# A mixture-of-experts decoder step on one core: expert inputs selected by matmuls on chip, and three visits with 64 places

## The chip, the core and the metric

The kernel runs on one core of a Trainium2 chip. The core has a matrix engine (PE, with PEld for its weight loads), a vector engine (DVE), a scalar engine (ACT), GpSimd (POOL) and SyncE (SP), and 16 DMA engines that all queues share. The metric is the device time of one execution in microseconds (us). A piece of weights here is 2048 KB or less, and a "visit" is the work of one expert.

## The reference

One step of a two-layer decoder on 256 prompt tokens and 8 sample tokens (264 in all, width 1024): retention and a dense SwiGLU, then an HGRN2 mixer and a top-2-of-8 expert SwiGLU with hidden width 3584. All is fp32. The change lies in the expert part:

```python
def moe_swiglu(h, router, wg, wu, wd):
    probs = jax.nn.softmax((h @ router).astype(F32), axis=-1)
    vals, idx = lax.top_k(probs, TOP_K)
    vals = vals / jnp.sum(vals, axis=-1, keepdims=True)
    combine = jnp.sum(jax.nn.one_hot(idx, N_EXPERTS, dtype=F32) * vals[..., None], axis=-2)
    out = jnp.zeros(h.shape, F32)
    for e in range(N_EXPERTS):
        out = out + combine[..., e:e + 1] * swiglu(h, wg[e], wu[e], wd[e]).astype(F32)
    return out.astype(h.dtype)
```

Here h is the RMS-normed row with a gain. Over the reference's inputs the router chooses the eight experts 74, 68, 61, 70, 66, 55, 72 and 62 times (528 choices).

## The kernel before

**The mixers.** The first 683 us compute both mixers and the dense layer with the tokens along the free dimension. The last product there (`hw`) adds into `xT`; PE turns `xT` back into token rows `x_tok` (`finished_rows`) and forms the router's logits, DVE chooses two experts a token, and PE counts, by a triangular matmul, the place of each token within its expert (`rk`).

**The visits.** A visit holds C = 96 places (TG = 3 groups of 32) for the tokens of one expert, the last visit only 64 (two groups, `GROUPS`); DVE puts the least-chosen of the experts 1 to 7 into the last visit (`order_of_visits`). If an expert has more tokens than places, all eight visits are repeated in another round of the loop `Fori(0, rounds)`; the trace shows one round. A visit (loop over `e`) uses 24 pieces of weights in the order of `EXPERT`: pieces 0 to 15 are gate and up, in two halves of the hidden width, of 1792 KB each; pieces 16 to 23 are the down projection, three of 2048 KB and one of 1024 KB in each half. `rows_times` multiplies `xe` (the expert's inputs, turned so that channels lie on partitions, 8 x 96 places) by a gate or up piece: 2 k-slices x groups x 4 matmuls of 32 columns, four at a time in the array. `hidden_times` does the same with `hide` and a down piece. ACT applies silu (L1312), DVE multiplies (L1947) and turns the hidden rows (L1949). Each fp32 matmul stands as two rows in the trace.

**The weights.** SP loads the pieces into 8 slots (`MOE_SLOT`). Before a piece it waits until PE is done with the piece eight earlier (`reused`, semaphore `w_used`). Piece 18 of the last visit is loaded ahead during visit 1, into a place of its own (`ahead_slot`).

**The expert inputs.** For visit 0, PE selects rows by matmuls (36 of them, `gsel` as weights, 256 columns of `x_tok` moving), DVE multiplies by the gain (L1907) and turns them (L1899). For the other visits DVE writes normed rows `h_tok` (`normed_rows`, L1894), POOL scatters each token's row to its two places of the DRAM tensor `y_scr` (L962, six indirect DMAs), SP loads 128 rows of it for the next visit (`load_rows`, L832, at piece 12 of a visit, or piece 2 of the last), and DVE turns them in blocks of 32 x 256 (L1954, 8 or 12 a visit) at the end of the visit.

**The results.** ACT and DVE take a visit's result out of PSUM in the next visit (L1303, L1941) and ACT stores it in `y_scr`. After piece 17 of the last visit POOL gathers two rows a token (L969, `w_seen`); DVE adds them by weight (`early`, L1969). The last visit's result goes from PSUM to tokens by a selection matmul (`select`), DVE adds it (`late`, L1976), and `final` norms and scales the rows (L1986), which SP stores.

Of the kernel before, what the change touches and what calls it, by code (L numbers as in the profile page):

```python
# [48 lines left out]
C_LAST = 64  # L49
GROUPS = [TG] * (NE - 1) + [C_LAST // 32]  # L50
# [248 lines left out]
def hybrid_step(nc, ins, outs):  # L299
    FILL, BANKS = fills()  # L300
    with ExitStack() as ctx:
# [42 lines left out]
        sel_mem = sb("last_selection", [P, 896], F32R)  # L344
# [112 lines left out]
        h_tok = part(earena, 3072, 3, D)  # L457
        gsel = part(earena, 6144, 3, C)
        ahead_slot = earena[:, 3072:3072 + PIECE]
        act_g = part(earena, 7168, TG, GW)  # L460
        first_rows = part(earena, 7168, TG, 256)

        y_out = part(cst, CONST["ones"][0], TG, 512)
        g_row = cst[:, CONST["lvl"][0] - 128:CONST["lvl"][1]]
        frees_at = 9264
        gfin = cst[:, CONST["dmask"][0]:CONST["dmask"][1]]
        x_row = g_row
        xe = part(xe_mem, 0, KD, C)

        g_group = part(hide_mem, 384, 1, 256)  # L470
        hide = [part(hide_mem, h * HB * C, HB, C) for h in range(2)]
        squares_at = [h_tok[:, 0, :], xe_mem[:, 0:D], hide_mem[:, 0:D]]
# [20 lines left out]
        last_sel = part(sel_mem, 0, TG, NT)  # L493
# [8 lines left out]
        oab = part(earena, RB + 184, 2, 3, 8)  # L502
# [6 lines left out]
        counts = part(earena, RB + 452, 8)  # L509
        visit_8 = part(earena, RB + 460, 8)  # L510
        visit_of = part(earena, RB + 500, 2, 3)
        to_last = part(earena, RB + 506, 2)
# [54 lines left out]
        x_pad_ok = sem("sample_rows_padded")  # L567
        h_tok_ok = sem("normed_rows_ready")
# [26 lines left out]
        x_scattered = sem("x_rows_scattered")  # L595
        x_row_in = sem("expert_x_rows_in")
        xe_ok = sem("expert_x_ready")
        gate_ok = sem("expert_silu_ready")
# [181 lines left out]
        X_AT, X_AT_LAST = 12, 2  # L780
# [20 lines left out]
        def _(sp):  # L801
# [29 lines left out]
            def load_rows(i):  # L831
                sp.dma_start(x_row, y_scr[bass.ds(i * C, P), :]).then_inc(x_row_in, 16)  # L832

            for t in range(EP):
                if t == X_AT:
                    sp.wait_ge(x_scattered, 96)
                    load_rows(2)
# [21 lines left out]
            def visit(v, i):  # L859
# [34 lines left out]
        def _(pool):  # L894
# [53 lines left out]
            freed(pool, ("lv", 4, 3))  # L948
            pool.dma_start(g_row, ins["norm_ffn_g"][1].partition_broadcast(P)).then_inc(rows_in, 16)
            filled(pool, ("hvar", 0))  # L950
            for c in range(4):
                pool.dma_start(g_group[32 * c:32 * c + 32, 0, :],
                               ins["norm_ffn_g"][1][256 * c:256 * c + 256].partition_broadcast(32)).then_inc(rows_in, 16)
# [390 lines left out]
        def _(dve):  # L1344
# [568 lines left out]
            for t in range(3):  # L1913
                normed_rows(t)
# [742 lines left out]
```

## Time and profile before

| | us |
|---|---|
| median of 3 runs | 1541.55 (1540.8 to 1542.12) |
| the profiled execution | 1543.34 |
| its span in the trace | 1541.5 |
| start of visit 0 in it | 682.6 |
| visits 0 to 7 | 682.6 to 1526.7 |
| after the last product of visit 7 | 14.8 |

The page shows PE busy for 98% of the span, over half of it in the visits, where the DMA engines are busy too. The rows of a visit repeat, so one visit can be read for several. A matmul's row overlaps its neighbours', so that the pace of PE is read from starts, not from the length of one row. "issue" means that the engine waited for nothing that the profile shows.

### The profile page before, as it was taken

What the parts mean: (1) busy time and instruction counts of PE and PEld (TensorE: products, weight loads), DVE (VectorE), ACT (ScalarE), POOL (GpSimd) and SP (SyncE); (2) the same over time, 40 slices, a digit from 0 to 9 for tenths busy, and PEclk for the clock granted to TensorE, in tenths of its full rate; (3) what the DMA queues carried; (4) which work ended last, traced back from release to release, by engine and by line L of the source; (5) the groups of instructions that cost most, each with busy time, mean ns of one, the idle gap of its engine ahead of it and who ended that gap; (6) DMA issues with size and microseconds to landing.
All of it is one profiled execution on the core that took longest, in us unless ns stands there. A gap on an engine that the chain in (4) does not pass through costs nothing.

```text
span 1541.5 us, 31601 instructions
## 1 busy us (share of the span) xinstructions
PE 1511.2 (98%) x14136; PEld 903.7 (59%) x14136; DVE 643.9 (42%) x1025; ACT 404.6 (26%) x613; POOL 86.6 (6%) x118
## 2 busy tenths in 40 slices
PE   9999999999999999999999999999999999999986
PEld 7888889999999999864333333333333333333322
DVE  7566878677656897551301301301311312112034
ACT  4444666544455547530000010010010000000001
POOL 1122221000000011010000000000000000000001
PEclk9999999999999999999999999999999999999998
DMA  9687786688656545569999999999999999999995
GB/s 373 223 287 268 258 291 216 201 275 280 223 179 209 199 164 196 233 234 418 426 408 427 426 425 427 424 419 429 405 424 430 395 423 427 401 427 416 423 427 249
DMA packets 136937, 515.88 MB, mean 335 GB/s; under 512 B 6488, under 2 KB 58912, under 8 KB 128480
## 3 DMA queue, kind: packets, MB, share of 16 engines
q1 hardware_dynamic: 116672, 450.03, 73.7%
q0 software_dynamic: 15968, 57.97, 10.2%
q10 hardware_dynamic: 4160, 5.84, 1.1%
q8 instruction: 112, 1.84, 0.4%
q14 instruction: 25, 0.20, 0.0%
HBM read 473.48 MB, written 40.34 MB: 333 GB/s over the span
## 4 chain that ended last, share of the span: by engine, by line
issue 53%; PE 37%; DVE 3%; ACT 1%; DMA 1%; POOL 0%; POOLq 0%; ACTq 0%; DVEq 0%
PE ps L2020 35%; DMA ring<-y_scr,expert_arena 1%; PE ps L2233 1%; DVE ring L1458 0%; POOL y_scr L962 0%; ACT ring_low_parts L1019 0%; DVE expert_arena L1969 0%; PE ps L2360 0%; DVE expert_arena L1986 0%; DVE ring_low_parts L1408 0%; DVE expert_arena L1976 0%; DVE expert_arena L1894 0%; ACT arena L1196 0%; PE ps L2481 0%; DVE arena L1748 0%
## 5 line engine op out<-in xcount | busy, mean ns | idle before, releaser
L2020 PE MATMUL ps<-ring,expert_x_turned 128*32 128x448 f32 x5152 | 488.8, 539 | 1.6 <-issue 0.8
L2020 PEld LDWEIGHTS ps<-ring,expert_x_turned 128*32 128x32 f32 x5152 | 169.5, 110 | 318.1 <-issue 316.2
L2020 PE MATMUL ps<-normed_high,ring_low_parts 128*128 128x264 f32 x1344 | 267.2, 290 | 0.4 <-DVE normed_low L1392 0.4
L2020 PE MATMUL ps<-ring,expert_hidden_turned 128*32 128x512 f32 x2360 | 257.4, 595 | 6.0 <-DMA ring<-in_moe_w_down 6.0
L1408 DVE TENSOR_TENSOR ring_low_parts<-ring,ring_low_parts 128x1024 fp32r<-128x1024 f32 (+3 forms) x184 | 209.1, 1142 | 84.6 <-ACT ring_low_parts L1019 84.2
L1019 ACT CAST ring_low_parts<-ring 128x1024 fp32r<-128x1024 f32 (+3 forms) x184 | 180.8, 983 | 222.9 <-PE ps L2020 214.3
L1947 DVE TENSOR_TENSOR expert_arena<-expert_arena,ps 128x1344 f32<-128x1344 f32 (+1 forms) x16 | 23.9, 1496 | 481.8 <-PE ps L2020 481.8
L2020 PEld LDWEIGHTS ps<-normed_high,ring_low_parts 128*128 128x128 f32 x1344 | 214.9, 189 | 5.4 <-issue 4.2
L2020 PEld LDWEIGHTS ps<-ring,expert_hidden_turned 128*32 128x32 f32 x2360 | 76.8, 110 | 184.0 <-issue 174.4
L2020 PE MATMUL ps<-normed_low,ring_low_parts 128*128 128x264 f32 x640 | 159.3, 284 | 0.0
L2020 PE MATMUL ps<-h_parts,ring_low_parts 128*128 128x264 f32 x1056 | 129.6, 285 | 0.0
L2020 PEld LDWEIGHTS ps<-h_parts,ring_low_parts 128*128 128x128 f32 x1056 | 129.0, 188 | 0.5 <-issue 0.4
L2020 PEld LDWEIGHTS ps<-normed_low,ring_low_parts 128*128 128x128 f32 x640 | 120.6, 188 | 0.6 <-issue 0.2
L1303 ACT COPY cst<-ps 32x1536 f32<-32x1536 f32 (+1 forms) x16 | 22.1, 1378 | 370.4 <-PE ps L2020 370.1
L1312 ACT ACTIVATE expert_arena<-ps 128x1344 f32<-128x1344 f32 (+1 forms) x16 | 19.9, 1244 | 365.9 <-PE ps L2020 365.9
L1941 DVE TENSOR_TENSOR cst<-ps,cst 32x1536 f32<-32x1536 f32 (+1 forms) x16 | 26.9, 1684 | 182.9 <-ACT cst L1303 182.1
L2020 PE MATMUL ps<-mixed_high,ring_low_parts 128*128 128x264 f32 x384 | 74.6, 291 | 1.7 <-DVE normed_high L1793 1.6
L2020 PE MATMUL ps<-expert_piece_slot,expert_x_turned 128*32 128x448 f32 x736 | 72.1, 539 | 1.1 <-DMA expert_piece_slot<-in_moe_w_up 1.1
L2020 PE MATMUL ps<-hidden_high,ring_low_parts 128*128 128x264 f32 x352 | 64.2, 284 | 0.0
L2020 PEld LDWEIGHTS ps<-mixed_high,ring_low_parts 128*128 128x128 f32 x384 | 61.0, 191 | 4.0 <-issue 2.5
L1954 DVE STREAM_TRANSPOSE expert_x_turned<-cst 32x256 f32<-32x256 f32 x92 | 58.8, 639 | 1.1
L2020 PEld LDWEIGHTS ps<-hidden_high,ring_low_parts 128*128 128x128 f32 x352 | 54.5, 188 | 0.0
(294 smaller groups left out, 1157.0 us busy)
## 6 DMA issues: line engine op xcount, KB each, us to landing
ring<-in_moe_w_gate SPq DMA_DIRECT2D x64, 1792.0 KB, 12.0
ring<-in_moe_w_down SPq DMA_DIRECT2D x47, 2048.0 KB, 13.6
ring<-in_moe_w_up SPq DMA_DIRECT2D x48, 1792.0 KB, 12.2
expert_piece_slot<-in_moe_w_up SPq DMA_DIRECT2D x16, 1792.0 KB, 13.0
ring<-in_ret_w_in SPq DMA_DIRECT2D x8, 2048.0 KB, 11.1
ring<-in_state_retention POOLq DMA_DIRECT2D x32, 512.0 KB, 6.6
out_ret_s<-ring POOLq DMA_DIRECT2D x32, 512.0 KB, 4.0
ring<-in_hg_w_in SPq DMA_DIRECT2D x8, 2048.0 KB, 8.0
```

The lines of the kernel that those rows point to most:

```text
L1019: A.copy(block_hi(n), block_raw(n)).then_inc(fw_hi_ok, 1)
L1303: A.copy(y_out[64 * q:64 * q + 32, 0:m], ps[64 * q + 32:64 * q + 64, b:b + m, :]).then_inc(y_half_ok, 1)
L1312: A.activation(act_g[:, 0:m], ps[:, b:b + m, 0:GW], ACT.Silu).then_inc(gate_ok, 1)
L1408: V.tensor_tensor(block_lo(n), block_raw(n), block_hi(n).bitcast(F32), ALU.subtract).then_inc(fw_lo_ok, 1)
L1941: V.tensor_tensor(y_out[z, 0:m], ps[z, b:b + m, :], y_out[z, 0:m], ALU.add).then_inc(y_ok, 1)
L1947: V.tensor_tensor(act_g[:, 0:m], act_g[:, 0:m], ps[:, b:b + m, 0:GW], ALU.mult).then_inc(mult_ok, 1)
L1954: j = V.transpose(xe[32 * c:32 * c + 32, :, 32 * t:32 * t + 32], x_row[32 * t:32 * t + 32, 256 * c:256 * c + 256].rearrange("p (f b) -> p ...
L2020: return nc.tensor.matmul(out, lhsT, rhs, start=first, stop=last)
L2233: i = nc.tensor.transpose(bank(("vb", u))[:, P * e:P * e + P], col, ident)
```

## The change

The inputs of every visit are now formed as those of visit 0 were, by matmuls on chip, and already turned.

- **gather_x on PE.** 24 matmuls (8 channel slices x 3 blocks of tokens): the weights are 128 columns of `x_tok`, taken eight elements (32 bytes) apart, the moving operand is the selection `gsel` (96 or 64 places). For visit 0 they replace the 36 of before. For every next visit, and after visit 7 too, they stand behind piece 17 of the visit (`GATHER_BEHIND`), into PSUM banks 6 and 7.
- **DVE.** `selection` (three small operations) after the first hidden half of each visit, and `take_expert_x` (two multiplies by the gain, out of PSUM) at its end, in place of the 8 or 12 transposes. The ranks of all experts are kept (`rank_at`), and `order_of_visits` swaps three pairs of columns of a table of ten numbers an expert.
- **Gone.** `normed_rows`, the six scattering DMAs, the row loads of SP and its wait for the scatter, the two loads of gain rows (one small load of the gain instead), a fill of `x_tok` on POOL.
- **64 places in three visits.** `FEW = (7, 4, 1)`: visits 1, 4 and 7 hold the three least-chosen of experts 1 to 7 (55, 61 and 62 tokens) with two groups in place of three. Another round is run if the third of them has over 64.
- A shorter `keep_busy` after visit 0's selection, and a wait of PE for `xe_ok` before the final selection.

```diff
-C_LAST = 64
-GROUPS = [TG] * (NE - 1) + [C_LAST // 32]
+C_FEW = 64
+FEW = (7, 4, 1)
+GROUPS = [C_FEW // 32 if v in FEW else TG for v in range(NE)]
...
-                    if t == (X_AT if v < NE - 1 else X_AT_LAST):
-                        sp.wait_ge(xe_ok, i + 1)
-                        load_rows(i + 2)
...
-            pool.wait_ge(h_tok_ok, 3)
             pool.wait_ge(rows_ok, 1)
-            pool.wait_ge(xe_ok, 1)
-            for t in range(3):
-                m = P if t < 2 else NS
-                for w in range(2):
-                    pool.indirect_dma_start(y_scr[:, :], bass.IndirectOffsetOnAxis(ap=rowi[0:m, w, t:t + 1], axis=0),
-                                            h_tok[0:m, t, :], None).then_inc(x_scattered, 16)
...
+            def selection(v, numbers):
+
+                for t in range(3):
+                    m = P if t < 2 else NS
+                    i = V.tensor_scalar(gsel[0:m, t, 0:32 * GROUPS[v]], numbers[0:m, 0:32 * GROUPS[v]],
+                                        rank_at[0:m, t, v:v + 1], rstd_tok[0:m, t:t + 1], ALU.is_equal, ALU.mult)
+                i.then_inc(sel_ok, 1)
...
+                for n, v in enumerate(FEW):
+                    link(V.tensor_scalar(swap_at, expert_at, fewest_expert[:, n:n + 1], None, ALU.is_equal))
+                    at = swap_at.unsqueeze(1).to_broadcast([P, 10, 8])
+                    link(V.tensor_tensor(swap_tmp, by_visit, at, ALU.mult))
...
+            def take_expert_x(v, q, o):
+
+                w = 32 * GROUPS[v]
+                return V.tensor_tensor(xe[:, 4 * q:4 * q + 4, 0:w], o[:, 0:4 * w].rearrange("p (k s) -> p k s", k=4),
+                                       moe_gain[:, 4 * q:4 * q + 4].unsqueeze(2).to_broadcast([P, 4, w]), ALU.mult)
...
-                    dve.wait_ge(x_row_in, i * 16 + 16)
-                    for t in range(GROUPS[(e + 1) % NE]):
-                        for c in range(4):
-                            j = V.transpose(xe[32 * c:32 * c + 32, :, 32 * t:32 * t + 32],
-                                            x_row[32 * t:32 * t + 32, 256 * c:256 * c + 256].rearrange("p (f b) -> p b f", b=KD))
-                    j.then_inc(xe_ok, 1)
+                        if h == 0:
+                            selection((e + 1) % NE, places)
+                            dve.wait_ge(sel_ok, i + 2)
+                            rank_of_further_round((e + 1) % NE)
...
+                    for q in range(2):
+                        dve.wait_ge(x_full, i * 2 + (q + 1))
+                        j = take_expert_x((e + 1) % NE, q, ps[:, 6 + q, :])
+                    j.then_inc(xe_ok, 1)
...
+            def gather_x(q, o, w):
+
+                for k in range(4 * q, 4 * q + 4):
+                    for s in range(3):
+                        m = P if s < 2 else NS
+                        i = mm(o[:, w * (k % 4):w * (k % 4) + w],
+                               x_tok[0:m, s, :].rearrange("t (p k) -> t k p", k=KD)[:, k, :], gsel[0:m, s, 0:w],
+                               s == 0, s == 2)
+                return i
...
+                        if t == GATHER_BEHIND:
+                            if e == 0:
+                                pe.wait_ge(last_sel_ok, r * TL + (1 + TL))
+                            pe.wait_ge(sel_ok, n + 2)
+                            for q in range(2):
+                                gather_x(q, ps[:, 6 + q, :], 32 * GROUPS[(e + 1) % NE]).then_inc(x_full, 1)
```

On PE, the down pieces 16 to 23 of visit 0 and the first pieces of visit 1, before:

```order
L2020 MATMUL ps<-ring,expert_hidden_turned 32x512 x48
L2591 REGISTER_ALU
L2020 MATMUL ps<-ring,expert_hidden_turned 32x512 x36
L2586 REGISTER_ALU
L2020 MATMUL ps<-ring,expert_hidden_turned 32x512 x72
L2020 MATMUL ps<-expert_piece_slot,expert_hidden_turned 32x512 x12
L2576 REGISTER_ALU
L2577 ISA
L2591 REGISTER_ALU
L2020 MATMUL ps<-ring,expert_x_turned 32x448 x48
```

and in the changed kernel:

```order
L2007 MATMUL ps<-ring,expert_hidden_turned 32x512 x48
L2591 REGISTER_ALU
L2592 REGISTER_ALU
L2007 MATMUL ps<-expert_arena 128x64 x24
L2582 REGISTER_ALU
L2007 MATMUL ps<-ring,expert_hidden_turned 32x512 x36
L2577 REGISTER_ALU
L2007 MATMUL ps<-ring,expert_hidden_turned 32x512 x72
L2007 MATMUL ps<-expert_piece_slot,expert_hidden_turned 32x512 x12
L2568 ISA
L2582 REGISTER_ALU
L2007 MATMUL ps<-ring,expert_x_turned 32x448 x32
```

The 24 matmuls of `gather_x` have moved in between pieces 17 and 18, and visit 1 has 32 matmuls in two pieces where it had 48.

On DVE, the second half of a visit and its end (here visit 2, between the two takes of a result), before:

```order
L1947 TENSOR_TENSOR expert_arena<-expert_arena,ps 128x1344
L1949 STREAM_TRANSPOSE expert_hidden_turned<-expert_arena 128x3x14x32
L1946 REGISTER_ALU
L1947 TENSOR_TENSOR expert_arena<-expert_arena,ps 128x1344
L1948 REGISTER_ALU
L1949 STREAM_TRANSPOSE expert_hidden_turned<-expert_arena 128x3x14x32
L1951 ISA
L1954 STREAM_TRANSPOSE expert_x_turned<-cst 32x8x32 x12
```

and in the changed kernel:

```order
L1932 TENSOR_TENSOR expert_arena<-expert_arena,ps 128x1344
L1934 STREAM_TRANSPOSE expert_hidden_turned<-expert_arena 128x3x14x32
L1822 TENSOR_SCALAR expert_arena<-visit_tables,expert_arena 128x96 x2
L1822 TENSOR_SCALAR expert_arena<-visit_tables,expert_arena 8x96
L1938 REGISTER_ALU
L1828 TENSOR_SCALAR visit_tables<-visit_tables 128x3
L1931 REGISTER_ALU
L1932 TENSOR_TENSOR expert_arena<-expert_arena,ps 128x1344
L1933 REGISTER_ALU
L1934 STREAM_TRANSPOSE expert_hidden_turned<-expert_arena 128x3x14x32
L1889 TENSOR_TENSOR expert_x_turned<-ps,expert_arena 128x384 x2
```

The transposes at the end have given way to two multiplies, and the selection stands behind the first hidden half.

## Rows read from the trace of the kernel before

**Rows 1.** Page: what the DMA engines moved, in 40 slices of the span.
```profile
GB/s 373 223 287 268 258 291 216 201 275 280 223 179 209 199 164 196 233 234 418 426 408 427 426 425 427 424 419 429 405 424 430 395 423 427 401 427 416 423 427 249
```

**Rows 2.** Busy time by stretch (visits 0, 2 and 7; visit 7 to 1520).
```profile
core 0: us, PE busy (x) PEld busy (x) DVE busy (x) ACT busy (x) POOL busy (x), PEclk, DMA share, GB/s
682.60:794.10 111.50, 110.86 (x1114) 39.51 (x1118) 25.84 (x46) 3.99 (x4) 5.65 (x6) 1.00 0.98 402
...
902.30:1010.50 108.20, 108.20 (x1110) 35.87 (x1106) 19.21 (x18) 5.44 (x4) 0.00 (x0) 1.00 1.01 424
...
1443.30:1526.70 83.40, 75.50 (x744) 23.92 (x736) 20.97 (x22) 6.96 (x8) 5.59 (x6) 0.98 0.97 407
1443.30:1520.00 76.70, 68.80 (x696) 21.99 (x692) 16.67 (x18) 6.38 (x7) 5.59 (x6) 1.00 1.01 426
```

**Rows 3.** Waits of PE, 1443 to 1542 us: line, releaser, us, times, longest.
```profile
PE ps L2020 <- DMA ring<-in_moe_w_down: 6.0, 4, 2.5
PE ps L2020 <- DMA expert_piece_slot<-in_moe_w_up: 1.1, 1, 1.1
```

**Rows 4.** Waits of SP's queue, 690 to 1542 us.
```profile
SPq L829 <- PE ps L2020: 694.7, 180, 5.5
```

**Rows 5.** DMAs of visit 2 (902.3 to 1010.5 us): issues, size, us to landing.
```profile
DMA packets 5997, 45.89 MB, mean 424 GB/s; under 512 B 439, under 2 KB 439, under 8 KB 4961
...
q8 instruction: 9, 0.15, 0.5%
...
cst<-y_scr SPq DMA_DIRECT2D x1, 512.0 KB, 16.0
y_scr<-cst ACTq DMA_DIRECT2D x2, 192.0 KB, 7.6
```

**Rows 6.** Timeline of PE in visit 7: start, length, rows, idle before.
```profile
1467.38 18.22 PE L2020 MATMUL ps<-ring,expert_x_turned 128*32 128x448 f32 x192
1486.39 0.96 PE L2020 MATMUL ps<-ring,expert_x_turned 128*32 128x448 f32 x8 [0.79 <-DMA ring<-in_moe_w_up]
```

**Rows 7.** The same, from piece 17 of visit 7 on.
```profile
1500.40 3.64 PE L2020 MATMUL ps<-ring,expert_hidden_turned 128*32 128x512 f32 x32 [1.18 <-DMA ring<-in_moe_w_down]
1503.86 3.62 PE L2020 MATMUL ps<-expert_arena,expert_hidden_turned 128*32 128x512 f32 x32
```

**Rows 8.** Timeline of PE before visit 0.
```profile
673.80 1.59 PE L2020 MATMUL ps<-expert_arena,cst 128*128 128x24 f32 x12
...
676.60 4.09 PE L2020 MATMUL ps<-expert_arena 128*32 128x256 f32 x72
...
682.63 0.96 PE L2020 MATMUL ps<-ring,expert_x_turned 128*32 128x448 f32 x8 [0.23 <-issue]
```

**Rows 9.** Timeline of DVE around the start of visit 0.
```profile
679.47 0.69 DVE L1907 TENSOR_TENSOR expert_arena<-ps,expert_hidden_turned 128x512 f32<-128x512 f32 x1 [0.34 <-PE ps L2020]
680.19 1.12 DVE L1899 STREAM_TRANSPOSE expert_x_turned<-expert_arena 128x512 f32<-128x512 f32 x1
681.23 0.39 DVE L1907 TENSOR_TENSOR expert_arena<-ps,expert_hidden_turned 128x256 f32<-128x256 f32 x1
681.65 0.64 DVE L1899 STREAM_TRANSPOSE expert_x_turned<-expert_arena 128x256 f32<-128x256 f32 x1
...
690.40 2.46 DVE L1941 TENSOR_TENSOR cst<-ps,cst 32x1024 f32<-32x1024 f32 x2 [0.59 <-issue]
```

**Rows 10.** Timeline of SP: the first issues of visit 1's pieces.
```profile
763.57 13.22 SPq L829 DMA_DIRECT2D ring<-in_moe_w_gate  x4
```

**Rows 11.** Groups by line and form, 676 to 1541 us: the transposes of expert inputs.
```profile
L1954 DVE STREAM_TRANSPOSE expert_x_turned<-cst 32x256 f32<-32x256 f32 x92 | 58.8, 639 | 1.1
```

**Rows 12.** Instructions of one slot: the landings of its DMAs.
```profile
DMA to landing us min/median/max: 9.9/12.8/29.2
```

**Rows 13.** Chain that ended last, in order of time: a gathered block, and the last step.
```profile
1508.40 16.44 DMA ring<-y_scr,expert_arena
...
1537.93 1.27 DVE expert_arena L1986
```

More of the change, by code:

```diff
@@ L501, in hybrid_step @@
         ixf = part(earena, RB + 160, 3, 8)
-        oab = part(earena, RB + 184, 2, 3, 8)
+        by_visit = part(tables, 0, 10, 8)
+        expert_at, rank_at = by_visit[:, 0], by_visit[:, 1:4]
+        oab = part(tables, 32, 2, 3, 8)
+        swap_tmp = part(tables, 80, 10, 8)
+        places = part(tables, 240, C)
+        moe_gain = part(earena, RB + 48, 8)
+        fewest_in = part(earena, RB + 56, 8)
+        fewest = part(tables, 176, 8)
+        fewest_ix = tables[:, 184:192].bitcast(U32)
+        fewest_expert = part(tables, 192, 8)
+        swap_at = part(tables, 200, 8)
+        swap_of = part(tables, 208, 10)
+        swap_by = part(tables, 218, 10)
+        few_off = part(tables, 234, 2, 3)
         mm_ = part(earena, RB + 232, 3, 8)
@@ L778, in moe_bank @@
             return 3 * ((e + group) % 2)
-        X_AT, X_AT_LAST = 12, 2
+        GATHER_BEHIND = 17
         AHEAD, AHEAD_VISIT, AHEAD_AT = 18, 1, 8
@@ L1897, in turn_rows @@
-            def turn_rows(rows, t0=0, t1=TG):
-                return V.transpose(xe.rearrange("p k (t s) -> p t k s", t=TG)[:, t0:t1],
-                                   rows[:, t0:t1].rearrange("p t (f b) -> p t b f", b=KD))
-            dve.wait_ge(rows_in, 96)
-            order_of_visits()
-            for q in range(2):
-                t0, t1 = 2 * q, min(2 * q + 2, TG)
-                filled(dve, ("first", q))
-                frees(V.tensor_tensor(first_rows[:, t0:t1], bank(("first", q))[:, 0:256 * (t1 - t0)].rearrange("p (t n) -> p t n", n=256),
-                                      g_group.to_broadcast([P, t1 - t0, 256]), ALU.mult), ("first", q))
-                freed(dve, ("first", q))
-                i = turn_rows(first_rows, t0, t1)
@@ L1912, in _ @@
+            dve.wait_ge(rows_in, 32)
+            for q in range(2):
+                filled(dve, ("first", q))
+                i = take_expert_x(0, q, bank(("first", q)))
+                frees(i, ("first", q))
+            freed(dve, ("first", 1))
+            dve.sem_inc(xe_ok, 1)
+            order_of_visits()
             rows_of_tokens()
-            for t in range(3):
-                normed_rows(t)
-            dve.wait_ge(rows_ok, 1)
-            V.tensor_copy(row_g, rowi)
+            rank_of_further_round(0)
@@ L2597, in _ @@
                         i.then_inc(w_used, 1)
+                        if t == GATHER_BEHIND:
+                            if e == 0:
+                                pe.wait_ge(last_sel_ok, r * TL + (1 + TL))
+                            pe.wait_ge(sel_ok, n + 2)
+                            for q in range(2):
+                                gather_x(q, ps[:, 6 + q, :], 32 * GROUPS[(e + 1) % NE]).then_inc(x_full, 1)
                         if e == 0 and t == 2 * GROUP_PIECES - 1:
@@ L2610, in _ @@
             pe.wait_ge(last_sel_ok, rounds * TL + 1)
+            mm(ps[0:32, last_bank[2], 0:1], ident[:, 0:32], ident[:, 0:1])
+            pe.wait_ge(xe_ok, last + 2)
             mm(ps[0:32, last_bank[2], 0:1], ident[:, 0:32], ident[:, 0:1])
```

127 lines of the change are left out of this document (48 added, 79 removed).

## The prediction

> **What bounds the kernel now.** I read the slices of the page first: up to some 685 us the DMA engines move 164 to 287 GB/s in most slices, from there to the end about 425 [rows 1]. The change lies behind that point, so the visits decide. Next the busy time by visit: each visit of 96 places lasts 108.2 us with PE busy through all of it at a granted clock of 1.00, and the DMA engines busy too, at 424 GB/s in visit 2. Visit 7, with 64 places, lasts 83.4 us with PE busy for 75.5 [rows 2]. The waits say who leads. SP's queue waited 694.7 us for PE to free slots [rows 4], so in the long visits PE leads and the weights follow; in visit 7 PE waited for weights, 6.0 us and 1.1 us in the two largest entries [rows 3].
>
> **The two rates.** Six pieces of visit 7 took PE 18.2 us [rows 6], 3.0 us each, two thirds of the 4.5 us of a piece with three groups (108.2 us hold 24 pieces, [rows 2]). A visit of 64 places is thus 2/3 of 108.2 = 72.1 us of PE. The weights of a visit are 16 pieces of 1792 KB, six of 2048 KB and two of 1024 KB, 44.0 MB. The stream's full rate is that of visit 7 up to 1520 us, 426 GB/s [rows 2], and 44.0 MB take 103.4 us at it. With results (two DMAs of 192 KB, or 128 KB after a short visit) and instruction fetches (0.15 MB and a little more) [rows 5] it is 104.7 us. So a long visit is PE's by 3.5 us, and a short one is the stream's by 32 us, from which the stock in the slots is taken. That stock shows in visit 7: PE ran from 1443.3 through 14 short pieces before its first wait at 1486.4 [rows 2, 6]; the stream needs 4.3 us for a piece of 1792 KB, so PE used up 14 x 1.3 = 18 us of stock.
>
> **Part 1, the matmuls that select.** In a visit 24 matmuls are added, 48 rows, with 128 columns of weights each. The nearest rows on PE are the 12 of the counting step, also 128 columns of weights with a narrow moving operand, 8 to 24 columns: the first starts at 673.80 and the group ends at 675.4, with 0.27 us of drain in it, so 0.11 us a row [rows 8]. Nothing in the array takes longer for 96 moving columns: 256 columns in a quarter of the array took 4.09 us for 72 rows, four side by side [rows 8]. That gives 48 x 0.11 = 5.3 us, and 5.6 with the changes of shape of the array around it, none of which shows idle time at 676.60. What these rows do not have is the step: the weights are read 32 bytes apart. The nearest rows for that are on DVE: its multiply of contiguous rows took 0.69 us for 512 and 0.39 us for 256 elements, 1.2 ns an element more, the transpose that walks its input 32 bytes apart 1.12 and 0.64 us, 1.9 ns [rows 9]. The bounds are 5.3 us, and 128 x 1.9 ns = 0.24 us a row or 11.5 us a gather. I take 5.6: PE's own rows count more than those of an operation that also transposes, and nothing of the trace shows PE slowed by a pattern.
>
> The row first: DVE pays 1.9 against 1.2 ns an element where it walks 32 bytes apart [rows 9]. The Trainium skill, "SBUF — State Buffer", section "Door 1: The DMA port swizzle", says that SBUF has 16-byte lines, that two hits a line are needed for full bandwidth, and that four fp32 elements are the widest free stride. By that rule each of the 128 weights here is a line of its own, and it speaks against the change; for PE no row of the trace bears it out or denies it. It is the second case below, by its own rows.
>
> **Part 2, the start of visit 0.** Before: selection at 676.60, DVE's last transpose, first product at 682.63 [rows 8, 9]. Now 48 rows end at about 682.1 and one multiply of 384 elements (0.55 us between the two of rows 9) takes the place of two multiplies and two transposes, of which 1.4 us lay behind PE's end. First product at 682.9, +0.3 us.
>
> **Part 3, visit 0.** It was 111.5 us [rows 2], now 111.5 + 5.6 = 117.1. The slots are full at its end, so the gather behind piece 17 delays the freeing of slots and with it the stream by the same 5.9 us in all.
>
> **Part 4, from visit 1 on.** PE would need 5.6 us more in each visit and 36.1 less in visits 1 and 4: a long visit 113.8, a short one 77.7. The stream needs 104.7 for either. A short visit uses up 27 us, more than the stock of 18, so PE runs into the stream in visit 1. Visits 2 and 3 rebuild 2 x 9.1 = 18.2, just what fits, so the slots do not fill up before visit 4 takes it all again, and so on to the end. The stream hence sets the time from visit 1 on. Its bytes from the first piece of visit 1 to piece 17 of visit 7: six visits and 18 pieces of weights and the one loaded ahead, 299.9 MB; seven results, 2.5; instructions 1.2; together 303.6 MB, of which 301.8 lie behind the first piece. That first piece was issued at 763.57 [rows 10], now 769.5; the quickest landing of a piece is 9.9 us [rows 12], then 301.8 MB / 426 GB/s = 708.5 us. While the slots are still full in the first eight issues, 1 us is lost to PE's slower down pieces. Piece 17 of visit 7 starts at 769.5 + 9.9 + 708.5 + 1 = 1488.9, where it started at 1500.4 [rows 7]: 11.5 us earlier.
>
> **Part 5, the end.** After piece 17 POOL gathers rows and DVE adds and norms them, and this chain ended last [rows 13]; it hangs on the start of piece 17 and on the same DMAs as before. PE has the useless gather of visit 7 there, 5.6 us. Pieces 17 to 23 with it make 5 x 3.46 + 2 x 1.73 + 5.6 = 26.4 us; before, with waits for weights, 1526.7 - 1500.4 = 26.3 [rows 2, 7]. So it takes the place of waiting, and the last 41.1 us stay.
>
> **Costed at nothing.** The eight row loads and the scatter (512 KB each, and 2.2 MB) only free the stream, which the bytes above count; SP's waits for them go, and what SP then waits for is PE or the slots. DVE's 58.8 us of transposes [rows 11] lay beside PE; in their place are six small operations a visit. DVE's work on visit orders before its loop grows from some 25 to some 55 operations of about 0.2 us, 6 us, less 3.7 us for the normed rows. It ended at 692.9 with the first result [rows 9] and must end before PE's piece 4 at 701: some 3 us are left as cover. If it is gone, the excess counts once. SP needs the visit order only at 763.6.
>
> **Sum.** The profiled span was 1541.5 us and the median of the runs 1541.55, so that the span stands for the runs; the profiled execution's own 1543.34 has 1.8 us around it. 1541.5 - 11.5 = 1530. A measurement of this kernel can tell about 0.2% (3 us) from no change.
>
> **Rival 1: the strided weights are slow, and PE leads again.** From a gather of G us on, PE no longer runs into the stream in the long visits. PE then needs 3.3 us for the extra of visit 0, 5 x 108.2 + 3 x 72.1 = 757.3, and 8 G; it still waits in each short visit, where 18 pieces before the gather take 55 us of PE and 79 us of stream less 18 of stock, about 5.5 us, three times; and visit 0 starts G - 5.1 later than 682.6. The end of visit 7 is 682.6 + 3.3 + 757.3 + 16.5 + 9 G - 5.1 = 1454.6 + 9 G, against 1526.7. It decides at G = 8.0 us, 0.17 us a row. With 1.6 times the row of Part 1, as DVE shows, G is 8.5 and the time 1546; with 0.24 us a row 1573; a middle G of 10 gives 1559. For it: DVE's rows. Against: PE's weight load is no slower than its other rows anywhere in the trace, but none there is strided.
>
> **Rival 2: no difference.** The stream may not hold 426 GB/s for 700 us; in the visits paced by PE it moved 395 to 430, 418 on average [rows 1], which is just what these ask for, so the trace does not show it. At 420 Part 4 is 10 us longer, and the time 1540. G near 7.5 gives the same.
>
> **Rival 3: another round.** If one of the short visits' experts had over 64 tokens, all visits would be run again, some 840 us more. The reference's counts, 55, 61 and 62, speak against it.
>
> **How the numbers follow.** Forecast 1530, own range 1526 to 1536: 0.57. Rival 1: 0.33, of it 0.25 up to 1566. Rival 2: 0.09, of which 0.02 ends faster and 0.01 slower by over 0.2%. Rival 3: 0.01. Faster 0.59, same 0.06, slower 0.35. The range from 1526 to 1566 leaves out 0.03 below and 0.09 above.
>
> **What would show it.** Right: visit 1 begins near 800, PE waits for weights in visits 1, 4 and 7 alone or nearly so, some 27 us in all, the 48 rows of a gather span 5.3 to 6 us, and DMA holds 426 GB/s in visits 2, 3, 5 and 6. Wrong: weight loads of the gather over 0.17 us apart (rival 1), PE busy without waits in the long visits at some 118 us each, DMA near 420 with PE waiting (rival 2), or a wait of PE for DVE at piece 4 of visit 0.

## The result, and the profile after

| | before | after |
|---|---|---|
| median, us | 1541.17 (1539.97 to 1542.12) | 1625.32 (1623.04 to 1629.19) |
| ratio | 1 | 1.0549, 95% interval 1.0527 to 1.0571 |
| span of the profiled execution | 1541.5 | 1627.4 |
| start of visit 0 | 682.6 | 691.7 |
| visits 0 to 7, us each | 111.5, 6 x 108.2, 83.4 | 128.4, 100.4, 125.1, 125.3, 93.9, 125.2, 125.5, 97.8 |
| behind the last product of visit 7 | 14.8 | 14.1 |

The change makes the kernel slower by 5.5%, where the forecast was 1530. Going through the table, the start takes +9.1 us, visit 0 +16.9, the four later visits of 96 places +16.9, +17.1, +17.0 and +17.3, visit 7 +14.4; only visits 1 and 4 are shorter, by 7.8 and 14.3, and the tail by 0.7. The sum is the 85.9 us of the spans.

The page of the changed kernel first: busy tenths of PE, granted clock of TensorE and what the DMA engines moved, in 40 slices. The last of the three answers [rows 1].

```profile
PE   9999999999999999999998999999999999999987
PEclk9999999999999999899899898998897998997987
GB/s 369 213 263 296 291 261 226 210 258 280 179 215 194 173 171 225 203 306 407 233 408 429 424 425 422 304 428 369 274 427 427 425 429 328 402 430 228 399 430 120
```

PE is busy everywhere, and yet the stream, which in [rows 1] stood near 425 to the end, has holes (233, 304, 274, 228), and the clock drops in slice after slice. Next the busy time by stretch, columns as in [rows 2]: visits 0, 1, 2, 3, 4 and 7.

```profile
691.70:820.10 128.40, 128.36 (x1159) 48.81 (x1162) 22.67 (x71) 3.86 (x3) 0.00 (x0) 0.92 0.81 319
820.10:920.50 100.40, 92.34 (x788) 35.79 (x784) 11.10 (x12) 4.70 (x4) 0.00 (x0) 0.92 1.01 422
920.50:1045.60 125.10, 125.10 (x1160) 46.05 (x1156) 12.57 (x12) 4.59 (x4) 0.00 (x0) 0.95 0.94 388
1045.60:1170.90 125.30, 125.30 (x1156) 46.11 (x1152) 13.33 (x12) 5.45 (x4) 0.00 (x0) 0.93 0.87 356
1170.90:1264.80 93.90, 90.50 (x788) 35.10 (x784) 11.11 (x12) 4.70 (x4) 0.00 (x0) 0.91 1.01 426
1515.50:1613.30 97.80, 92.42 (x793) 35.38 (x786) 16.29 (x17) 6.96 (x8) 5.61 (x6) 0.90 0.83 344
```

In the long visits PE is busy for all of the time and the stream moves only 388 and 356 GB/s; in visits 1 and 4 it runs at 422 and 426 and PE has idle time. PE leads in the long visits: Rival 1's picture. The waits say the same, first PE's, then SP's, 690 to 1627 us (line, releaser, us, times, longest), which answer [rows 3, 4]:

```profile
PE ps L2007 <- DMA ring<-in_moe_w_down: 9.5, 6, 2.0
PE ps L2007 <- DMA ring<-in_moe_w_up: 3.4, 3, 2.4
...
SPq L833 <- PE ps L2007: 791.3, 180, 27.0
```

With 2.7 and 1.3 us more in two further rows PE waits 16.9 us for weights in all, only in visits 1, 4 and 7, while SP's longest wait for a slot grew from 5.5 to 27.0 us. What PE does in that time stands behind piece 17. The timeline of PE in visit 2 (start, length, rows), and then the stretch of its first two channel slices and of the whole selection and the six pieces behind it (columns as in [rows 2]):

```profile
999.58 3.61 PE L2007 MATMUL ps<-ring,expert_hidden_turned 128*32 128x512 f32 x32
1003.11 15.00 PE L2007 MATMUL ps<-expert_arena 128*128 128x96 f32 x48
...
1003.11:1004.87 1.76, 1.76 (x10) 1.57 (x6) 0.00 (x0) 0.00 (x0) 0.00 (x0) 1.00 1.02 438
1004.87:1006.63 1.76, 1.76 (x7) 1.57 (x6) 0.00 (x0) 0.00 (x0) 0.00 (x0) 1.00 0.97 414
1003.11:1018.10 14.99, 14.99 (x56) 12.64 (x56) 0.56 (x1) 0.00 (x0) 0.00 (x0) 0.66 0.92 388
1018.10:1045.60 27.50, 27.50 (x245) 7.57 (x248) 0.56 (x1) 0.00 (x0) 0.00 (x0) 0.94 0.72 273
```

The 48 rows take 15.0 us, not 5.6; the nine selections span 14.3 to 15.2 us. The six rows of a slice take 1.76 us at a granted clock of 1.00, and eight slices at that pace are 14.1 us, so most of it is there before the clock moves. Then the clock falls: 0.66 over the selection, 0.94 over the pieces behind it, which take 27.5 us (25.75 at full clock, as a row further down shows). And as no slot is freed during the selection, the stream moves only 273 GB/s behind it.

### The profile page after: what moved, and what is told of

It is laid out like the page before. It is cut to its first block, busy times and chain, and to the rows that moved or that the text cites. A ratio compares the mean times of both kernels' runs of the same rounds, so it can differ in the third digit from the quotient of the medians.

```text
span 1627.4 us, 30811 instructions
## 1 busy us (share of the span) xinstructions
PE 1589.0 (98%) x13760; PEld 973.7 (60%) x13760; DVE 593.6 (36%) x1000; ACT 401.5 (25%) x613; POOL 78.4 (5%) x107
## 4 chain that ended last, share of the span: by engine, by line
PE 87%; DMA 5%; DVE 2%; ACT 1%; issue 1%; SPq 0%; ACTq 0%; DVEq 0%
PE ps L2007 86%; DMA ring<-in_moe_w_down 5%; PE ps L2220 1%; DVE ring L1437 0%; ACT ring_low_parts L999 0%; PE ps L2347 0%; DVE expert_arena L1973 0%; DVE ring_low_parts L1387 0%; DVE expert_arena L1963 0%; ACT arena L1176 0%; DVE arena L1727 0%; DVE expert_arena L1956 0%; PE ps L2468 0%; SPq L833 0%; ACT ring L1210 0%
## 5 line engine op out<-in xcount | busy, mean ns | idle before, releaser
L2007 PE MATMUL ps<-ring,expert_x_turned 128*32 128x448 f32 x4704 | 450.3, 543 | 4.9 <-DMA ring<-in_moe_w_up 3.4
L2007 PEld LDWEIGHTS ps<-ring,expert_x_turned 128*32 128x32 f32 x4704 | 144.0, 111 | 308.2 <-issue 301.7
L2007 PE MATMUL ps<-ring,expert_hidden_turned 128*32 128x512 f32 x2152 | 252.2, 629 | 9.5 <-DMA ring<-in_moe_w_down 9.5
L2007 PEld LDWEIGHTS ps<-ring,expert_hidden_turned 128*32 128x32 f32 x2152 | 67.5, 116 | 186.5 <-issue 171.6
L2007 PE MATMUL ps<-expert_arena 128*128 128x96 f32 (+3 forms) x432 | 133.2, 458 | 0.0
L2007 PEld LDWEIGHTS ps<-expert_arena 128*128 128x128 f32 (+1 forms) x432 | 113.2, 326 | 25.1 <-issue 17.8
L1889 DVE TENSOR_TENSOR expert_x_turned<-ps,expert_arena 128x384 f32<-128x384 f32 (+1 forms) x18 | 9.2, 513 | 181.0 <-PE ps L2007 181.0
L2007 PE MATMUL ps<-expert_piece_slot,expert_x_turned 128*32 128x448 f32 x672 | 66.0, 540 | 2.7 <-DMA expert_piece_slot<-in_moe_w_up 2.7
```

What stands on the lines that cost most here:

```text
L1889: return V.tensor_tensor(xe[:, 4 * q:4 * q + 4, 0:w], o[:, 0:4 * w].rearrange("p (k s) -> p k s", k=4), moe_gain[:, 4 * q:4 * q + 4].unsqu ...
L2007: return nc.tensor.matmul(out, lhsT, rhs, start=first, stop=last)
```

## The experiments

**The stream alone.** First, is the rest of the forecast right: would the weights set the time at 426 GB/s if the selections cost nothing? This kernel leaves out the selecting matmuls and the multiplies by the gain in all visits, so every expert works on the inputs of visit 0.

```diff
-                        if t == GATHER_BEHIND:
...
-                                gather_x(q, ps[:, 6 + q, :], 32 * GROUPS[(e + 1) % NE]).then_inc(x_full, 1)
...
-                        dve.wait_ge(x_full, i * 2 + (q + 1))
-                        j = take_expert_x((e + 1) % NE, q, ps[:, 6 + q, :])
-                    j.then_inc(xe_ok, 1)
+                    dve.sem_inc(xe_ok, 1)
```

> The changed kernel without the selecting matmuls and the multiplies by the gain in all eight visits (the inputs of visits 1 to 7 are left as visit 0's, so the experts' results are wrong in value; every weight is loaded and every product made). It tests the stream theory alone. Theory A (the selection's price on TensorE is the whole cause; without it the weight stream sets the time at 426 GB/s, as in Parts 4 and 5): the first piece of visit 1 is issued at 763.6 + 9.1 (the late start of visit 0 stays) = 772.7, so piece 17 of visit 7 starts at 772.7 + 9.9 + 708.5 + 1 = 1492, and with the last 41.1 us the span is 1533; DMA at 426 GB/s in every visit from 2 on. Theory B (the stream does not hold that rate): 420 GB/s or less, 1543 or more. Theory C (something else of the change costs too, such as the visits of 64 places): PE busy without waits in the long visits at more than 108.2 us each, 1550 or more.

Measured: 1538.59 us (ratio 0.9985, 0.9975 to 0.9994), span 1536.8. Visits 1, 2, 3 and 7:

```profile
802.70:893.60 90.90, 74.88 (x744) 22.96 (x737) 10.18 (x11) 5.93 (x6) 0.00 (x0) 1.00 1.01 426
893.60:1002.50 108.90, 108.63 (x1106) 35.70 (x1110) 11.17 (x10) 3.37 (x3) 0.00 (x0) 1.00 1.01 426
1002.50:1110.70 108.20, 108.20 (x1109) 35.87 (x1105) 12.40 (x10) 5.45 (x4) 0.00 (x0) 1.00 1.01 426
...
1425.60:1520.20 94.60, 77.08 (x745) 23.08 (x738) 12.65 (x13) 6.96 (x8) 5.62 (x6) 0.98 0.94 396
```

426 GB/s through the visits, long visits of 108.2 us, PE waiting in the short ones: theory A holds to 4 us, and B and C fall. The loss lies in the selections: those of the visits, and the one ahead of visit 0, which this kernel still has and which makes it start 9.7 us late.

**Stride and row count, one at a time.** Two properties of the 24 matmuls were not in the rows that priced them: the weights stand 32 bytes apart, and the third block of tokens has 8 rows where the others have 128. Each can be taken away. Adjacent weights:

```diff
-        moe_g = ins["moe_w_gate"][0].rearrange("e (p k) n -> p e k n", p=P)
+        moe_g = ins["moe_w_gate"][0].rearrange("e (k p) n -> p e k n", p=P)
...
-                               x_tok[0:m, s, :].rearrange("t (p k) -> t k p", k=KD)[:, k, :], gsel[0:m, s, 0:w],
+                               x_tok[0:m, s, P * k:P * k + P], gsel[0:m, s, 0:w],
```

The up weights (`moe_u`) and the gain are dealt in the same order.

> The changed kernel with channels dealt to partitions in blocks of 128 (gate and up weights, gain), so that the selecting matmuls read 128 adjacent columns of x_tok as weights. It computes the reference. Theory A (the 32-byte step is most of the price): weight loads 0.11 us a row, so 5.3 us of rows and some 2.6 us of changes between 128-row and 8-row operands, G = 7.9; visit 0 starts 2.8 us later than before the change, and the formula of Rival 1 gives 1454.6 + 9 x 7.9 = 1525.7 for the end of visit 7, which is just where it decides, so 1541, within 5 us. Theory D (the step costs nothing and TensorE's granted clock, which falls in each gather, is the price): the gather stays at 13 us or more and the time within 10 us of 1625. Theory E (any 128-row fp32 weight load with 96 moving columns costs 0.24 us): the same as D, with the clock at 1.00 or not.

And 128 rows everywhere, with zeros behind the eight:

```diff
-                        m = P if s < 2 else NS
+                        m = P
...
```

> The changed kernel with the third block of tokens (8 sample rows) filled up with zeros to 128 rows, the weights still 32 bytes apart. It computes the reference. Theory A: the two rows of a slice on 8 partitions cost as much as the others, 0.24 us, and only the changes of the row count go, 0.32 us a slice: G falls by 2.6 us and the time by 9 x 2.6 = 23 us, to 1602. Rival F (the changes cost nothing, and the longer rows are the start and end of a group in PSUM): G and the time as in the changed kernel, 1625. Rival G (a weight load of 128 rows is dearer than one of 8, and padding adds): above 1625.

Measured: adjacent 1585.84 us (ratio 1.0303, 1.0286 to 1.0321), filled up 1593.41 us (1.0346, 1.0328 to 1.0363). A channel slice of visit 1's selection at full clock, adjacent (the second slice) and then filled up (the first, with one load of the next), the filled-up selection of visit 2 as a whole, and the end of that of visit 0, all of it at half clock:

```profile
877.90:878.90 1.00, 1.00 (x7) 0.82 (x6) 0.00 (x0) 0.00 (x0) 0.00 (x0) 1.00 1.00 418
```

```profile
878.19:879.62 1.43, 1.43 (x10) 1.43 (x7) 0.00 (x0) 0.00 (x0) 0.00 (x0) 1.00 1.00 424
990.40:1002.15 11.75, 11.75 (x56) 11.57 (x56) 0.56 (x1) 0.00 (x0) 0.00 (x0) 0.65 1.00 426
784.62:786.23 1.61, 1.61 (x8) 1.49 (x7) 0.00 (x0) 0.00 (x0) 0.00 (x0) 0.50 0.00 0
```

A slice is 1.76 us with both faults, 1.43 without the changes of row count, 1.00 without the stride. Filled up, 48 loads are 11.75 / 48 = 0.24 us apart. Filled up, the selections take 11.7 us each, whatever the granted clock over them (0.63 to 0.75), and seven loads at a clock of 0.50 take 1.61 us, 0.23 each: strided loads are no slower at half clock. The adjacent ones take 8.8 to 11.7 us, shorter where less half clock falls in them (2.8 us of it in the shortest, 8.4 in the longest).

Theory A's prices hold, 0.24 us strided and 1.00 us a slice adjacent, which is 8.0 us a selection at full clock against the 7.9 expected. Its two times do not hold equally. Filled up it expected 1602 and got 1593: G fell by 3.1 us, not 2.6, and the six pieces behind took 26.8 us where they had taken 27.5. Adjacent it expected 1541 and got 1586, since it had the clock at 1.00: the half clock adds some 2.4 us to a selection and 1.6 us to the pieces behind it (27.3 against 25.7), and at 8 us all of that is on the path. So the clock, which rival D named, is a price of its own, though D's 13 us are wrong. E falls with D (adjacent loads of the same shape do not cost 0.24 us), and F and G fall with the 3.1 us that filling up takes off.

**The selection in four batches.** The clock might stay up if the slow loads came in short runs.

```diff
-                        if t == GATHER_BEHIND:
+                        if t in (17, 18, 19, 20):
...
+                            ks = range(per * a, per * a + per)
```

> The changed kernel with the selecting matmuls of a visit in four batches of two channel slices behind pieces 17, 18, 19 and 20 in place of one batch behind piece 17; the matmuls are the same. It computes the reference. Theory A, with the clock as a part of the price: in batches of 3.5 us the granted clock stays at 1.00 in the visits, which gives back some 1 us in the gather and 2 us behind it, 8 x 3 = 24 us, so 1601, and the batches sum to 14.1 us a visit. Rival H (the clock falls in short batches too, or the fall costs nothing since the loads are the limit): 1620 to 1630, or more if each change to the 32-row weights costs.

Measured: 1631.24 us (1.0593, 1.0575 to 1.0611). PE in visit 2, and that visit:

```profile
1004.55 3.59 PE L2007 MATMUL ps<-expert_arena 128*128 128x96 f32 x12
1008.08 5.36 PE L2007 MATMUL ps<-ring,expert_hidden_turned 128*32 128x512 f32 x48
1013.36 3.60 PE L2007 MATMUL ps<-expert_arena 128*128 128x96 f32 x12
1016.89 4.48 PE L2007 MATMUL ps<-ring,expert_hidden_turned 128*32 128x512 f32 x24
...
922.00:1049.30 127.30, 127.30 (x1156) 48.56 (x1152) 12.49 (x12) 4.59 (x4) 0.00 (x0) 0.96 0.93 385
```

Rival H came. The batches are what was expected, 3.5 us each, and the clock is down less (0.973 over the span against 0.952), but the time is not shorter. The rows show why: the 24 rows of a down piece at 1016.89 take 4.48 us, where a like piece at full clock takes 2.76. In one batch, most of the half clock lies on strided loads, which lose little by it (10.1 of 13.7 us of it in visit 2 of the changed kernel); in four batches it lies on products, which run at half their pace (8.8 of 10.2 us here). The visit is 127.3 us, of it 113.0 outside the batches; in the changed kernel 125.1 and 110.2.

**Both cures.** Adjacent weights and 128 rows, in one batch; then the same in four.

> The changed kernel with both cures: the weights of the selection 128 adjacent columns of x_tok, and the third block of tokens filled up to 128 rows. It computes the reference. Theory A (stride and changes of the row count are the price of the selection; the contiguous rows of the run before stood 0.11 us apart, each change cost 0.17 us more): the 48 rows of a selection take 48 x 0.11 = 5.3 to 6 us, visit 0 starts near 683, and the weight stream sets the time again as in the forecast. From the run without selections in the visits (1536.8 us, visit 0 at 692.3), which started 9 us later: 1536.8 - 9 + 6 in visit 0 = 1534, faster than the kernel before by 0.5%. Rival I (the granted clock falls in 5 us of selection as well, and some 10 us of half clock per visit cost 5 us): long visits of 119 us, 1555 or more.

> The kernel with both cures and, in the visits, the selection in four batches of two channel slices behind pieces 17 to 20. It computes the reference. Theory A: the batches sum to 5.4 us and, if the stream sets the time, it equals the kernel with both cures in one batch, 1534, within 3 us. If the clock falls there (Rival I), batches of 1.3 us keep it at 1.00, and this kernel is the faster of the two by what the clock takes.

Measured: 1533.3 us (ratio 0.9936, 0.9922 to 0.9949). Visits 1, 2 and 3, a selection, and the pieces behind it:

```profile
798.60:888.70 90.10, 79.84 (x788) 28.39 (x780) 11.29 (x13) 5.92 (x6) 0.00 (x0) 1.00 1.01 423
888.70:1004.40 115.70, 114.15 (x1156) 41.17 (x1160) 12.29 (x12) 3.37 (x3) 0.00 (x0) 1.00 1.01 426
1004.40:1118.20 113.80, 113.80 (x1156) 41.17 (x1152) 13.25 (x12) 5.45 (x4) 0.00 (x0) 1.00 1.01 420
973.10:978.65 5.55, 5.55 (x56) 5.46 (x56) 0.56 (x1) 0.00 (x0) 0.00 (x0) 1.00 1.02 437
978.65:1004.40 25.75, 25.75 (x245) 7.80 (x248) 0.56 (x1) 0.00 (x0) 0.00 (x0) 1.00 1.00 422
```

The selection takes 5.6 us, the clock stays at 1.00, and the time is 0.7 us from the 1534 expected; Rival I falls. This kernel is the one that the forecast described. Adjacent weights alone had taken 39 us off the changed kernel and filling up alone 32; both take 92, more than the sum, since with either alone the clock still falls and with both it does not. The four batches gave 1536.52 (0.9955, 0.9941 to 0.9968): no gain, as with the clock up there is nothing to win. They sum to 5.9 to 6.1 us a visit where one batch has 5.5; what makes the rest of the 3 us was not traced, and the intervals overlap.

**A long selection of cheap rows.** By Rival 1 the length of the selection decides, at any price per row: its line meets the time of before at 8.0 us. With cheap rows the selection can be made long by doing it twice:

```diff
+                                gather_x(q, ps[:, 6 + q, :], 32 * GROUPS[(e + 1) % NE])
                                 gather_x(q, ps[:, 6 + q, :], 32 * GROUPS[(e + 1) % NE]).then_inc(x_full, 1)
```

> Both cures, but each selection in a visit is done twice in the same place (the second result takes the place of the first; the output is the reference's). A visit's selection is then 10.6 us with cheap rows: it tests the price and the decision point of Rival 1 (8.0 us) apart from stride and row counts. Theory A: TensorE leads again in the long visits, 108.2 + 10.6 + some 1.5 of lower clock behind = 120 us each, and the time is near that of the kernel with padded strided rows (G = 11.7, 1590.7 us) less 6.4 us at visit 0 and 8 x 1.1: 1575. Theory J (not the length of the selection but the slow loads themselves disturb the stream or TensorE): within 10 us of the kernel with one selection, 1534.

Measured: 1569.96 us (1.0168, 1.0153 to 1.0184). A selection and visit 2:

```profile
980.12 10.96 PE L2011 MATMUL ps<-expert_arena 128*128 128x96 f32 x96
...
897.50:1016.80 119.30, 119.30 (x1207) 46.58 (x1202) 12.50 (x12) 4.59 (x4) 0.00 (x0) 1.00 1.01 426
```

108.2 + 11.0 us in each long visit and PE without a wait there: the rival's mechanism, with no stride in it, and Theory J falls. 5.4 us more in each of eight visits came out as 36.1 us of span (1568.5 - 1532.4), so some 7 us of the 43 were free, 0.9 us a visit. By this estimate PE leads from a selection of 5.5 + 0.9 = 6.4 us on. That is another point than the 8.0 us of Rival 1, at which its line is back at the 1526.7 of before, so that PE leads and nothing is won. The line itself is 7 us low here: the visits end at 1554.3, where it gives 1454.6 + 8 x 10.9 + 5.4 = 1547.2. Moved up by that much, it loses against before from 7.2 us on, again an estimate.

The clock stays at 1.00 although the selection is as long as those in which it fell. That prices the fallen clock. The adjacent version without filling up has selections in its visits that are 4.7 us shorter in all, and yet a span 15.3 us longer. Its eight stretches behind the selections take 16.4 us more (1.4 to 2.8 each), the first pieces of visit 0 take 1.7 more, visit 0 starts 5.1 later, and the pieces before the selections of the short visits, with less waiting for weights, take 3.1 less: 16.4 + 1.7 + 5.1 - 4.7 - 3.1 = 15.4. The first two terms, 18 us, are what the fallen clock costs there beside the selections.

**The worth of the short visits.**

```diff
-FEW = (7, 4, 1)
+FEW = (7,)
```

> Both cures, with 64 places in visit 7 alone (visits 1 and 4 hold 96 places as before the change). It computes the reference. It gives the worth of the two further short visits. Theory A: TensorE leads in visits 0 to 6, 108.2 + 5.6 us each; end of visit 6 = 683 + 111.5 + 5.6 + 6 x 113.8 = 1483, and the 98.2 us that before lay behind it give 1581, up to 1592 with 1.5 us of lower clock a visit: some 47 to 58 us above the kernel with three short visits. Theory K (the short visits give little, since the stream sets the time anyway): within 15 us of it.

Measured: 1581.71 us (1.0249, 1.0233 to 1.0265), long visits of 113.9 us without a wait. Theory A's 1581, and K falls. Cheap selections on PE with one short visit lose 2.5%, and the two further short visits win 48 us back, so the first half of the change cannot be judged without the second. The second alone, three short visits with the inputs still going through DRAM as before, was not run. So it is not shown how much of the gain the selections on PE bring. An estimate: the stream would carry the eight row loads of 512 KB [rows 5] as well, 4.2 MB or 9.8 us at 426 GB/s, on top of the run without selections less its late start, 1538.6 - 9.7, which is near 1539, against 1533 with both cures.

**What is left of the selection.** With both cures it costs where the slots are full, which is visit 0. So its place there should count, and elsewhere not.

```diff
-        GATHER_BEHIND = 17
+        GATHER_BEHIND = [23, 17, 17, 17, 17, 17, 17, 17]
...
```

> The kernel with both cures once more, as the base of the two that follow on the same chip: 1533, within 2 us.

> Both cures, and visit 0's selection for visit 1 behind its last piece (23) in place of piece 17; the others stay. It computes the reference. Theory L (what is left of the selections costs only where the slots are full and the stream waits for TensorE, and that is visit 0: pieces 18 to 23 free their slots 5.6 us earlier there, and the stream keeps that lead to the end): 5.6 us less, 1528. Theory M (the stream sets the time from its own start on, and the place of the selection does not matter): 1533; or 1534 to 1535 if the multiply by the gain, now with nothing between it and visit 1's first product, adds its 1 us.

> Both cures, and the selection behind piece 23 in visits 0 to 6 (visit 7 keeps its place). It computes the reference. Theory L: only visit 0's place counts, so 1528 as with visit 0 alone, within 2 us, since the 1 us of exposed multiply in the long visits is taken from the stock of weights. Theory N (each exposed multiply and each drain of the array adds to the end): 6 us slower than with visit 0 alone.

Measured, with the version with both cures at 1533.87 us (0.9948, 0.9934 to 0.9962) on the same chip: 1530.21 us (ratio to before 0.9928, 0.9915 to 0.9942) with visit 0 alone, 1531.21 (0.994, 0.9927 to 0.9954) with visits 0 to 6. SP in visit 0, first with both cures only and then with the selection behind piece 23 (start, length, issues):

```profile
762.49 18.86 SPq L834 DMA_DIRECT2D ring<-in_moe_w_gate  x4
785.99 10.67 SPq L834 DMA_DIRECT2D ring<-in_moe_w_up  x3
```

```profile
762.44 13.22 SPq L834 DMA_DIRECT2D ring<-in_moe_w_gate  x4
780.30 10.67 SPq L834 DMA_DIRECT2D ring<-in_moe_w_up  x3
```

The pieces are issued 5.7 us earlier, of which 3.7 us reach the end: theory L in direction and place, though it expected 5.6; M (1533) falls. Visit 1's first product now waits 0.69 us for the multiply by the gain, and its pieces free their slots that much later; the other 1.3 us were not traced and are within what a median can tell. With the other visits' selections moved too the time is 1 us more, within the intervals, so N's 6 us did not come. The version with visit 0 alone is the fastest of all.

**The price of one change of row count.** A last run keeps the 8-row block and halves the changes by going through the blocks backwards in every second slice.

```diff
-                    for s in range(3):
+                    turn = (0, 1, 2) if k % 2 == 0 else (2, 1, 0)
+                    for s in turn:
...
-                               s == 0, s == 2)
+                               s == turn[0], s == turn[2])
```

> Adjacent weights as in the run with blocks of 128, no filling up of the third block, but every second channel slice takes the blocks of tokens in reverse order, so that a selection has 8 changes of the row count in place of 16. It computes the reference. Theory A (each change costs 0.17 us): the selection takes 48 x 0.11 + 8 x 0.17 = 6.7 us where the granted clock is 1.00. If the clock stays there, the stream sets the time and only visit 0 counts, 2 x 1.1 us above the filled-up version: 1536. If the clock still falls in the selections, 7 to 9 us each and some 1.5 us behind them, near or over the point of 8.0 us: 1540 to 1560. Rival O (not the changes but the narrow 8-row operands themselves are slow, 0.28 us for the pair): the selection takes as long as without the reversal, 8.0 us at full clock, and the time is that run's, 1586.

Measured: 1549.81 us (1.0062, 1.0049 to 1.0076). The selections of visits 2, 3 and 4:

```profile
977.00:983.90 6.90, 6.90 (x56) 6.04 (x52) 0.56 (x1) 0.00 (x0) 0.00 (x0) 1.00 1.02 437
1092.20:1100.50 8.30, 8.30 (x56) 7.53 (x56) 0.42 (x1) 0.00 (x0) 0.00 (x0) 0.78 1.00 424
1189.60:1196.50 6.90, 6.90 (x54) 6.03 (x51) 0.56 (x1) 0.00 (x0) 0.00 (x0) 1.00 1.02 433
```

6.9 us at full clock: (6.9 - 5.55) / 8 = 0.17 us a change, and Rival O falls. The time is in the band expected for a clock that still falls, 1540 to 1560: it falls in three of the eight selections in visits, those of visits 0, 3 and 6. These are the ones whose moving operand has 64 columns; in the other five it has 96, and the clock stays. Where it fell a long visit takes 118.2 us, else 115.4 to 115.9.

## Why the prediction was wrong, step by step

**Part 1 is the step that failed.** It gave the selection 5.6 us out of bounds of 5.3 and 11.5, because "PE's own rows count more than those of an operation that also transposes, and nothing of the trace shows PE slowed by a pattern". No row of PE was strided, so the trace could not show it either way; the absence of a row was taken as evidence. PE's strided loads stand 0.24 us apart, just the upper bound from DVE's rows in [rows 9]; that the two engines agree so closely may be chance, as no run tells why either is slower. The rule of the Trainium skill, "SBUF — State Buffer", section "Door 1: The DMA port swizzle", that was set beside the row (at 32 bytes each weight is a line of its own) pointed the right way: loads of 128 weights take 0.24 us strided and 0.11 us adjacent here.

**The changes of row count were in no bound.** "5.6 with the changes of shape of the array around it" left out those inside it, 16 a selection. A sign of them was in [rows 8]: the 12 counting rows include four on 8 partitions, and 11 spacings of 0.11 us with 0.27 of drain make 1.48 us, where the group has 1.59. Divided by 12 the change was spread over the rows. Here it costs 0.17 us a change with adjacent weights (2.7 us a selection); with strided ones the selections are 2.6 to 3.5 us longer than without the changes.

**The clock was not foreseen at all.** It was read as 1.00 in the visits before and not asked what the slow loads would do to it. It fell in each of the nine selections. In the changed kernel it costs little inside them, where loads set the pace, and 1.8 to 2.8 us a long visit behind them.

**Rival 1 was right in mechanism and short in price.** Long visits busy without waits and the short ones waiting: both seen, for a chance of 0.33. Its 8.0 us is the point of no gain, not the one from which PE leads; the runs put the two near 7.2 and 6.4. Its line 1454.6 + 9 G was given up to G = 11.5 and 1573. With the mean G of 14.8 it gives 1587.8 for the end of visit 7, which is 1613.3. The 25.5 us between are 9 in the four later long visits (125.1 to 125.5 against 123.0), 2 in visit 0, 15 in the three short ones (292 against 277) and -0.6 at the start. Of the 15, waits for weights are only 0.4 (16.9 against 3 x 5.5). The pieces behind the selections take 58.7 us where they take 51.6 at full clock, which is 7.1, and some 3.4 more go to two stretches of half clock, 3.4 us each, ahead of the selections of visits 1 and 7. The last 4 us have no cause shown; they are there at full clock too, since the doubled cheap selection has 274.1 us in the short visits, of it 20.7 of waits, against 3 x (72.1 + 10.9) = 249.0 of work. So 1625 lies 52 us above the 1573 of the rival's dearest row: 9 x 3.3 = 30 for selections longer than 11.5 us, mostly by the changes of row count, and the 25.5 just listed, less 0.7 in the tail and 2.1 by which the profiled span lies above the median. The upper end of the range, 1566, was below even that dearest row.

**Right were** Part 4's stream (426 or 427 GB/s in visits 1 to 6 without the selections, 419 to 426 with both cures) and, with G at 5.6, its sum: with both cures piece 17 of visit 7 starts at 1491.4 against the 1488.9 of Part 4, visit 1 at 798.6 against "near 800", PE waits 25.4 us for weights against 27 (5.6 of it in visits 2 and 5, where none was expected), and the span is 1532.4 against 1530. In Part 5 the last 41.1 us are 41.0 there; in the changed kernel they are 54.2, since the selection of visit 7 no longer takes the place of waiting. Part 2 was short: visit 0 starts 1.0 us later with both cures, where it said 0.3, and 9.1 in the changed kernel. The cover of 3 us for DVE's visit order held: in the changed kernel PE waits for no DVE operation in visit 0. Rivals 2 and 3 did not come.

## What to carry to other kernels

Price an operation by rows that have its access pattern and its sequence, not only its shape; where none exists, take both ends of the bound as cases of equal weight, and say what would have to be true for the cheap one. Where an engine and a stream of loads take turns in setting the pace, work out from which price of the added work the engine leads again (here some 6.4 us a visit) and from which the change loses (some 7.2), and weigh the forecast by how sure the price is to stay below them. If a selection by matmuls pays only in one layout of the weights, choose the layout of the other operand to suit: here the channels of two weight tensors dealt in blocks of 128, which alone left a loss of 3.0%, and 8 rows filled up to 128 with zeros, which alone left 3.5%, together turned a loss of 5.5% into a gain of 0.5 to 0.6%, and 0.7% with one selection moved.

## What the runs showed of the hardware

- A load of 128 x 128 fp32 weights that stand 32 bytes apart takes 0.24 us where adjacent ones take 0.11 (5.5 us for 48), and the 0.24 is the same at half of TensorE's clock (11.7 us for 48 at a granted clock of 0.63 to 0.75 over them; 0.23 at 0.50).
- A change between operands on 128 and on 8 partitions costs 0.17 us with adjacent weights (6.9 us a selection with 8 changes, 5.55 with none).
- The granted clock fell while the profile shows PE busy without a gap: in every undivided selection with strided weights, in every one with adjacent weights and 16 changes of row count, and in the kernel with 8 changes in the three of the visits' eight selections where 64 columns move. With strided weights in four batches it fell in every visit too, mostly between the batches. It never fell in a selection with adjacent weights and no changes, not even in 11 us of them. What decides it was not measured.
